# Rotary tables moved behind the first z tile, values stored by heads, unit weights loaded in halves, store waits moved

## What is computed

```
h = rmsnorm(x, pre_norm_w)                            # 2048 x 1024
q, k, v, z_att, b, c, u, z_conv, g_att, g_conv = split(h @ w_in)
q, k = partial_rotary(q, positions), partial_rotary(k, positions)   # 8 heads of 64, first 16 dims turned
a = softmax(q1 k1^T / 8) - lam * softmax(q2 k2^T / 8)  # 4 head pairs, chunk-causal mask (positions // 64)
att = rmsnorm(a @ v) * 0.8 * silu(z_att)               # v: 4 heads of 128
cv = b * conv3_causal(c * u) * silu(z_conv)
m = sigmoid(g_att + bias0) * (att @ w_att_out) + sigmoid(g_conv + bias1) * (cv @ w_conv_out)
x = x + rmsnorm(m @ w_out, post_norm_w)
```

## Time and profile before

| what | value |
|---|---|
| median of three executions | 1808.36 us (1807.6 to 1809.15) |
| the profiled execution | 1808.52 us |
| its span, first to last instruction | 1806.7 us |
| PE matmul busy | 1758.4 us, 97% of the span |
| PE weight load, DVE, ACT, POOL busy | 1466.7, 893.8, 580.3, 89.0 us |
| mean granted TensorE clock | 0.991 of full speed |
| DMA | 328.90 MB, mean 182 GB/s |
| PE's waits, largest groups | 12.4 us for `at_lo`, 11.1 us for unit weights, 8.1 us for the first x tile |

### The profile page before, as it was taken

One profiled execution on the slowest core, in us unless ns is written; L12 is line 12 of the kernel. 1 busy time (PEld: TensorE's weight loads), 2 busy tenths in 40 slices (PEclk: granted clock), 3 DMA queues, 4 the chain that ended last, 5 costly groups with the idle time before them and its releaser, 6 DMA issues.

```text
span 1806.7 us, 22424 instructions
## 1 busy us (share of the span) xinstructions
PE 1758.4 (97%) x8512; PEld 1466.7 (81%) x8512; DVE 893.8 (49%) x1903; ACT 580.3 (32%) x1039; POOL 89.0 (5%) x74
## 2 busy tenths in 40 slices
PE   7999999999999999999999999999899889999998
PEld 6887888888888888788887888888788768888887
DVE  5547244445334511276666666766576344424242
ACT  5423112121101111245444544444444333313231
POOL 0000000000000000111101111111001000000000
PEclk9999999999999999999999999999999999999999
DMA  6557346465503546965674778556856775453532
GB/s 233 164 189 314 129 163 210 163 210 167 178 18 129 162 118 174 265 219 186 198 211 151 221 233 271 181 180 208 248 158 185 227 281 172 120 181 111 175 105 76
DMA packets 149574, 328.90 MB, mean 182 GB/s; under 512 B 14801, under 2 KB 68049, under 8 KB 135889
## 3 DMA queue, kind: packets, MB, share of 16 engines
q1 hardware_dynamic: 149458, 327.37, 57.3%
HBM read 216.16 MB, written 111.16 MB: 181 GB/s over the span
## 4 chain that ended last, share of the span: by engine, by line
PE 83%; DMA 7%; ACT 3%; SPq 3%; DVE 2%; issue 2%; DVEq 0%; ACTq 0%
PE bank L937 18%; PE bank L938 18%; PE bank L939 18%; PE bank L1065 15%; PE bank L1027 5%; PE bank L999 3%; PE bank L1000 3%; PE bank L1010 2%; DMA raw<-in_w_in 2%; DMA ring<-gate_s 2%; SPq L669 2%; ACT e L1267 2%; DMA w<-split_s 1%; DMA gate_s<-gate_st 1%; DVE at_lo L1616 1%
## 5 line engine op out<-in xcount | busy, mean ns | idle before, releaser
L937 PE MATMUL bank<-ht,w 128*128 128x512 f32 x896 | 349.9, 390 | 3.0 <-issue 3.0
L938 PE MATMUL bank<-ht,w 128*128 128x512 f32 x896 | 349.7, 390 | 0.0
L939 PE MATMUL bank<-ht,w 128*128 128x512 f32 x896 | 349.5, 390 | 0.0
L1065 PE MATMUL bank<-ht,w 128*128 128x512 f32 x912 | 238.8, 396 | 4.0 <-DMA w<-split_s 4.0
L937 PEld LDWEIGHTS bank<-ht,w 128*128 128x128 f32 x896 | 168.8, 188 | 38.7 <-issue 3.4
L939 PEld LDWEIGHTS bank<-ht,w 128*128 128x128 f32 x896 | 168.9, 188 | 35.2
L938 PEld LDWEIGHTS bank<-ht,w 128*128 128x128 f32 x896 | 168.9, 188 | 35.1
L1065 PEld LDWEIGHTS bank<-ht,w 128*128 128x128 f32 x912 | 167.2, 189 | 36.7 <-DMA w<-split_s 4.6
L1580 DVE CUSTOM_DVE_ANT_0 e<-bank,zeros 128x512 f32<-128x512 f32 x192 | 125.0, 688 | 131.0 <-PE bank L1000 130.5
L1267 ACT ACTIVATE e<-e,nbias 128x128 f32<-128x128 f32 (+15 forms) x128 | 152.8, 1197 | 74.7 <-DVE nbias L1589 74.6
L1065 PE MATMUL bank<-hx,w 128*128 128x512 f32 x576 | 157.2, 401 | 7.0 <-DMA w<-split_s 7.0
(11 more groups left out here) (140 smaller groups left out, 2493.0 us busy)
## 6 DMA issues: line engine op xcount, KB each, us to landing
w<-split_s SPq DMA_DIRECT2D x62, 1024.0 KB, 5.4
split_s<-piece SPq DMA_DIRECT2D x24, 1024.0 KB, 5.0
q_st<-qk_s SPq DMA_DIRECT2D x128, 128.0 KB, 5.5
gate_s<-gate_st SPq DMA_DIRECT2D x64, 256.0 KB, 6.0
ring<-gate_s SPq DMA_DIRECT2D x64, 256.0 KB, 3.3
raw<-in_w_in SPq DMA_DIRECT2D x28, 512.0 KB, 5.7
ht_s<-ht SPq DMA_DIRECT2D x3, 4096.0 KB, 27.5
qk_s<-stage SPq DMA_DIRECT2D x48, 192.0 KB
```

The costliest lines, as they stand in the source:

```text
L937: nc.tensor.matmul(out, left[0], right[0], start=start, stop=False)
L938: nc.tensor.matmul(out, left[0], right[1], start=False, stop=False)
L939: return nc.tensor.matmul(out, left[1], right[0], start=False, stop=stop)
L1065: mm = nc.tensor.matmul(bank[2 + u % 2][:], unit_weights(u)[:, term // 2, k, :], h_slot(bb, k)[:, term % 2, :], start=i == 0, stop=i == PE ...
```

## The change

- DVE's table code becomes a function `tables()`, called in `before_tile(1)` after `tile_w(2)`; `chunk_ids()` moves to `before_tile(2)`. ACT's two sines move from `before_tile(0)` to `before_tile(1)`, after `tile_w(2)`.
- `v_s` becomes `[head, 128, row tile, hi/lo, 128]`. `stage` holds a v tile by heads, and a store writes runs of 1 KB instead of 2 KB. `load_v` is one DMA of 512 KB in which each partition reads one run of 4 KB, instead of two with 512-byte runs; `v_sl` has the matching order.
- A unit's weights come by two DMAs of 512 KB, k = 0 to 3 and k = 4 to 7, with a semaphore each. The first is issued when unit u - 2 is half done (new semaphore `unit_half`), the second when it is done. PE waits for the second only at its matmul 12.
- At the handover the load of unit 3 moves ahead of the last block's stores, the three further value loads move behind them, and the wait for all stores moves into the attention stage, to the end of unit 1, behind the store of unit 0.
- The first three `wa` loads are spread: behind units 49, 51 and 53.

```diff
-K_IN, V_IN, Q_IN = 2 * 16, 2 * 16, 4 * 16
+K_IN, V_IN, Q_IN = 2 * 16, 16, 4 * 16
-        v_s = scratch("v_s", [2, S, WIDTH])
+        v_s = scratch("v_s", [VH, P, NT, 2, VD])
-        v_sl = {i: held(f"v_sl{i}", [P, 2, QPB, VD], F32R, room) for i in (3, 0, 1, 2)}
+        v_sl = {i: held(f"v_sl{i}", [P, QPB, 2, VD], F32R, room) for i in (3, 0, 1, 2)}
+        def by_heads(i):
+            return stage[i % 4][:].rearrange("p s n -> p (s n)").rearrange("p (h s e) -> p h s e", h=VH, s=2)
-                sp.dma_start(v_s[:, i * P:(i + 1) * P, :].rearrange("s p e -> p s e"),
-                             stage[i % 4][:]).then_inc(stored[i % 4], 16)
+                sp.dma_start(v_s[:, :, i].rearrange("h p s e -> p h s e"), by_heads(i)).then_inc(stored[i % 4], 16)
-                for half in range(2):
-                    sp.dma_start(v_sl[i][:, half].bitcast(F32),
-                                 v_s[half, c:c + BLK, pair * VD:(pair + 1) * VD].rearrange("(t p) e -> p t e", p=P)
-                                 ).then_inc(v_loaded[i], 16)
+                sp.dma_start(v_sl[i][:].bitcast(F32), v_s[pair, :, c // P:c // P + QPB]).then_inc(v_loaded[i], 16)
-            def load_unit(u):
+            def load_unit(u, half=None):
                 if u >= 4:
-                    sp.wait_ge(unit_done, u - 1)
-                sp.dma_start(unit_weights(u)[:].bitcast(F32),
-                             split_s[u % GATE_TILES].rearrange("p s (k c) -> p s k c", k=KT)
-                             ).then_inc(first_in[u] if u < 2 else unit_w[u % 2], 16)
+                    if half:
+                        sp.wait_ge(unit_done, u - 1)
+                    else:
+                        sp.wait_ge(unit_half, u - 1)
+                for x in range(2) if half is None else (half,):
+                    sp.dma_start(unit_weights(u)[:, :, 4 * x:4 * x + 4].bitcast(F32),
+                                 split_s[u % GATE_TILES].rearrange("p s (k c) -> p s k c", k=KT)[:, :, 4 * x:4 * x + 4]
+                                 ).then_inc(first_in[u] if u < 2 else unit_w[2 * (u % 2) + x], 16)
             for i, (p, b) in enumerate(SEQ[-2 * NB:]):
+                if i == 7:
+                    sp.wait_ge(proj_done, AT[LINE - 1, 0] + 1)
+                    load_unit(3)
                 store_block(p, b)
...
                 if i == 6:
                     sp.wait_ge(proj_done, AT[LINE - 2, 0] + 1)
                     load_unit(2)
-                    for c in range(BLK, S, BLK):
-                        load_v(Plan(True), 0, c)
-            sp.wait_ge(proj_done, AT[LINE - 1, 0] + 1)
-            load_unit(3)
-            for i, s_ in enumerate(stored):
-                sp.wait_ge(s_, 16 * stored_in_all(i))
+            for c in range(BLK, S, BLK):
+                load_v(Plan(True), 0, c)
...
+                    if i == PER_UNIT // 2 - 1 and 4 <= u + 2 < UNITS:
+                        load_unit(u + 2, 0)
                     if i == PER_UNIT - 1:
                         if 4 <= u + 2 < UNITS:
-                            load_unit(u + 2)
+                            load_unit(u + 2, 1)
                         if u >= 1:
                             store_gate(u - 1)
+                        if u == 1:
+                            for x, s_ in enumerate(stored):
+                                sp.wait_ge(s_, 16 * stored_in_all(x))
                         if g % 2 == 1 and g < 12 and bb < NB - 1:
                             load_h(bb + 1, g // 2)
-                        if u == 3 * GATE_TILES + 1:
-                            for m in range(3):
-                                load_wa(m)
+                        if bb == NB - 1 and g in (1, 3, 5):
+                            load_wa(g // 2)
...
-                                pe.wait_ge(unit_w[u % 2], 16 * (u // 2))
+                                pe.wait_ge(unit_w[2 * (u % 2)], 16 * (u // 2))
...
+                        if i == PER_UNIT // 2 and u >= 2:
+                            pe.wait_ge(unit_w[2 * (u % 2) + 1], 16 * (u // 2))
...
-                        if i == PER_UNIT - 1:
+                        if i == PER_UNIT // 2 - 1:
+                            mm.then_inc(unit_half, 1)
+                        elif i == PER_UNIT - 1:
                             mm.then_inc(unit_done, 1)
...
             # ACT, before_tile(p)
-                if p == 0:
+                if p == 1:
                     act.wait_ge(cols_in, 48)
                     act.wait_ge(table_step, 14)
...
             # DVE, before_tile(p)
                 if 0 < p < LINE - 1:
                     tile_w(p + 1)
                 if p == 1:
+                    tables()
+                elif p == 2:
                     chunk_ids()
```

More of the change, by code:

```diff
@@ L471, in build @@
         att_stored = [sem(f"att_stored{i}") for i in range(2)]
-        unit_w = [sem(f"unit_w{i}") for i in range(2)]
+        unit_w = [sem(f"unit_w{i}") for i in range(4)]
         first_in = [sem(f"first_in{i}") for i in range(2)]
         ht_in = [sem(f"ht_in{i}") for i in range(KT // 2)]
-        ht_free, unit_done, gate_out = sem("ht_free"), sem("unit_done"), sem("gate_out")
+        ht_free, unit_half, unit_done, gate_out = sem("ht_free"), sem("unit_half"), sem("unit_done"), sem("gate_out")
         gate_stored = [sem(f"gate_stored{i}") for i in range(2)]
@@ L1025, in step @@
                         q0 = P if plan.causal and k == last else 0
-                        v = v_sl[plan.slot(G, k * P // BLK * BLK)][:, x // 2, k % QPB, :]
+                        v = v_sl[plan.slot(G, k * P // BLK * BLK)][:, k % QPB, x // 2, :]
                         return nc.tensor.matmul(bank[7][:, q0:QB], v, (at_lo if x == 1 else at_hi)[:, k, q0:QB],
@@ L1057, in gates @@
                             if u < 2:
-                                pe.wait_ge(first_in[u], 16)
+                                pe.wait_ge(first_in[u], 32)
                             else:
-                                pe.wait_ge(unit_w[u % 2], 16 * (u // 2))
+                                pe.wait_ge(unit_w[2 * (u % 2)], 16 * (u // 2))
                             if u >= 2:
                                 pe.wait_ge(gate_out, u - 1)
+                        if i == PER_UNIT // 2 and u >= 2:
+                            pe.wait_ge(unit_w[2 * (u % 2) + 1], 16 * (u // 2))
                         if bb and g == 0 and term == 0 and k % 2 == 0:
@@ L1185, in _ @@
                     act.wait_ge(stored[i % 4], 16 * (i // 4))
-                nc.scalar.activation(stage[i % 4][:, 0, :].bitcast(F32R), bank[4 + i % 4][:], ACT.Copy
+                nc.scalar.activation(by_heads(i)[:, :, 0].bitcast(F32R),
+                                     bank[4 + i % 4][:].rearrange("p (h e) -> p h e", h=VH), ACT.Copy
                                      ).then_inc(v_hi_out, 1)
@@ L1403, in _ @@
                 dve.wait_ge(v_hi_out, i + 1)
-                nc.vector.tensor_tensor(stage[i % 4][:, 1, :].bitcast(F32R), bank[4 + i % 4][:],
-                                        stage[i % 4][:, 0, :], ALU.subtract).then_inc(dve_done, 1)
+                nc.vector.tensor_tensor(by_heads(i)[:, :, 1].bitcast(F32R),
+                                        bank[4 + i % 4][:].rearrange("p (h e) -> p h e", h=VH),
+                                        by_heads(i)[:, :, 0], ALU.subtract).then_inc(dve_done, 1)
                 if i + 2 < NT:
```

29 lines of the change are left out of this document (15 added, 14 removed).

## The result

The changed kernel takes 1813.16 us, the median of seven executions (1810.76 to 1816.82). The kernel before took 1808.36 us in the seven beside them (1805.87 to 1809.77). The ratio is 1.0032 with a 95% interval of [1.0021, 1.0044]: slower by 0.32%, some 5 us. Forecast were 1806.8 us and no change, so it came out slower where no change was forecast, and the median lies 0.16 us above the top of the range. The profiled execution took 1813.16 us, with a span of 1811.3 us and a granted clock of 0.992.

A forecast was written before the change was run, and what follows sets the result against it. PE's matmuls fill 97% of the span, so only its stalls and lower clock could pay. Tables 13.5, v stores 0.5, gains 5.6, 2.4, 4.2 and 3.9, halves 0.5 sum to -1.6 us: 1806.8 us, 80% range 1798.5 to 1813.

The forecast's parts named there:

- tables: Before tile 3: PE stands 10.5 us behind DVE's moved table code, plus 3.0 us for the clock; cost 13.5 us.
- halves: Unit loads split in two: 60 more issues and later q, z and k loads; cost 0.5 us (0 to 2).
- B: Handover, units 2 and 3: idle plus clock 6.7 us, 1.1 us of stall left; gain 5.6 us (1 to 6.7).
- E: Unit 62: idle 2.80 us plus clock 1.5, in all 4.3; stall 0.4 left, gain 3.9 us (2.3 to 4.3).
- D: Change of keys, rounds 49 and 50: 5.9 us, stall 1.65 left, no clock fall; gain 4.2 us (2.8 to 5.9).
- Stores of v in 1 KB rows: Last v store, ahead of the raw tile on the queue: cost 0.5 us for tile 2 (0 to 1).
- second rival: Tables hidden after all, if tile 2's raw weights landed well before 160: -22.2 us, 1786; chance 0.07.
- A: Start of tile 2: idle 3.04 us plus clock 3.0, in all 6.0 us; gain forecast as nothing.
- third rival: Handover: SP's new wait for the `stage` stores makes q tiles late; total +5 us, 1813.4 us; chance 0.16.
- C: Change of keys, rounds 17 and 18: 4.1 us, stall 1.65 left, no clock fall; gain 2.4 us (1.2 to 4.1).
- first rival: Boundaries B to E clear whole, restart at tile 3 costs 1.2 us: -9.3 us, 1799.1 us; chance 0.31.
- The fourth: Clock falls in C and D as well and the halves cost SP 2 us: +2.5, up to +4; chance 0.05.

The follow-up runs named there:

- a3: The changed kernel with the load of tile 2's raw weights moved ahead of the three `ht` stores: 1793.65 us, ratio 0.9932 to the kernel before.
- b1: The changed kernel with tables, sines and `chunk_ids` at their old places and whole 1 MB unit loads: 1797.94 us, ratio 0.9954 to the kernel before.
- c1: The kernel before with only the unit loads in halves: 1809.56 us against 1805.92, ratio 1.0023.
- a2: The kernel before with only the tables, sines and `chunk_ids` moved to their new places: 1820.03 us, ratio 1.0073.
- a4: The kernel before with only the load of tile 2's raw weights moved ahead of the `ht` stores: 1804.01 us, ratio 0.9987.
- b3: The kernel before with only the handover's moves (unit 3's load, value loads, the wait for the stores): 1802.8 us, ratio 0.9983.
- b2: The kernel before with only the values stored by heads and one load per 512 keys: 1799.34 us, ratio 0.9959.
- a1: The changed kernel with tables, sines and `chunk_ids` back at their old places: 1800.61 us, ratio 0.9966 to the kernel before.
- c3: The changed kernel with tile 2's raw weights loaded ahead of the `ht` stores, halves throughout, run again: 1794.97 us, ratio 0.9940 to the kernel before.

## Why the prediction went wrong, point by point

From the profiles the change came out at +4.5 us where -1.6 was forecast. The cost of the tables was right to 0.6 us. Two steps failed. The halves were put at 0.5 us and cost 2.8 in one round that the sum did not contain. And the gains at B to E were put at 16.1 us and came to 11.7: a gate store that lands late, which the prediction took to be in time once SP comes earlier, held ACT at B, D and E, and E was priced from one profile.

**The tables: right.** Forecast: no gain at tile 2, a gap of 10.5 us before tile 3, PE back at 198, and 3.0 us for the clock. Measured: 10.00 us and 198.16. The 20-us stretches of the changed kernel (columns as in the earlier trace rows):

```profile
180.00:200.00 20.00, 10.00 (x41) 7.91 (x40) 12.68 (x17) 10.56 (x11) 0.00 (x0) 0.83 0.19 58
200.00:220.00 20.00, 20.00 (x83) 16.36 (x82) 11.56 (x15) 4.05 (x6) 0.00 (x0) 0.92 0.75 270
...
740.00:760.00 20.00, 18.80 (x87) 15.59 (x86) 3.68 (x15) 4.23 (x10) 1.57 (x1) 1.00 1.05 316
...
960.00:980.00 20.00, 18.15 (x107) 15.83 (x106) 11.47 (x32) 9.54 (x16) 1.57 (x1) 0.91 0.38 109
...
1300.00:1320.00 20.00, 17.52 (x110) 15.17 (x109) 11.03 (x31) 10.29 (x17) 1.57 (x1) 1.00 0.43 131
```

The clock cost 10.00 x 0.17 + 20.00 x 0.08 = 3.3 us where I had 3.0. Stores of v in 1 KB rows: tile 2 starts at 163.38 instead of 162.55, so 0.8 us for the 0.5 that I allowed. These readings add up to 14.1 us and the series has 13.4, where 14.0 was forecast. The second rival fell here for the reason given, and a3 shows that it hung on exactly that load. (Its sum had a slip: the terms of the prediction with A's 6.0 us and without the tables give -21.1 us, not -22.2.)

**The halves: the first step that failed.** I priced them at +0.5 us (0 to 2) and named the right mechanism (SP stops at every half unit, and what stands behind goes out later), but placed its cost nowhere. It falls in round 33, where keys, values, q tiles and unit weights are all loaded at once. SP's timeline of the changed kernel there:

```profile
1086.64 1.33 SPq L665 DMA_DIRECT2D k_sl<-qk_s  x2
1088.47 0.54 SPq L691 DMA_DIRECT2D w<-split_s  x1
1089.06 2.56 SPq L678 DMA_DIRECT2D q_st<-qk_s  x4
```

SP's timeline of the kernel before, the same q tiles:

```profile
1079.88 2.57 SPq L678 DMA_DIRECT2D q_st<-qk_s  x4
```

With the changed kernel 7.8 us behind, that is 1087.7 on its clock. They go out 1.4 us later, and the last of them takes 10.43 us to land (1091.01 to 1101.44), as PE's wait of 2.10 us shows, against 9.0 us in the kernel before. With the wait for `at_lo`, 1.57 us where it was 1.03, this is 2.6 us more idle time; by the series the round costs 2.8 us more than before, alone over the upper bound of the whole term. Whether SP's stop at the half unit or the smaller pieces ahead in the queue delay these tiles more, no run separates. Round 32 to 34 is no change of all four blocks of keys, so I never looked there. My list of places A to E was made of stalls that the kernel before *had*; a part that delays SP needs the places where it is only just in time.

The second half of the failed step is the reading of the earlier trace rows, "the second half is no later than the whole was". Both medians are over the whole span, quiet stretches included, and the 5.7 us are those of another load, the raw weights. The halves' own median is no worse (4.9 us in the changed kernel, 5.4 for whole loads before), yet where it counted it was: at the handover the first half of unit 2 took 14.7 us to land, the whole unit before 14.2. A half has 256 runs of 2 KB where the whole had 128 of 8 KB, and the page counts 164678 packets for 139079 with whole loads (b1). c1 measures all of it at +0.23% [0.14, 0.32], some 4 us. The Trainium skill (DMA: Bandwidth & Descriptors, Bandwidth) says to batch to 1 MiB or more. c1 agrees with it in direction, though it does not show that the size of the transfers is the cause, and the medians of the trace misled me. The estimate of 2.0 us by that page of the Trainium skill stood at E, while the loss that the traces show is in round 33.

**B: right in kind, 1.3 us too good.** Unit 3's wait is gone. But the order on SP is not what I drew. SP's timeline of the changed kernel at the handover:

```profile
742.65 8.54 SPq L691 DMA_DIRECT2D w<-split_s  x4
751.23 2.40 SPq L640 DMA_DIRECT2D qk_s<-stage  x3
...
756.41 0.33 SPq L730 DMA_DIRECT2D gate_s<-gate_st  x1
762.63 0.32 SPq L734 DMA_DIRECT2D hx<-ht_s  x1
763.00 0.54 SPq L691 DMA_DIRECT2D w<-split_s  x1
763.58 2.56 SPq L678 DMA_DIRECT2D q_st<-qk_s  x4
```

Four half loads held SP for 8.54 us, where a whole unit took 0.43 us to issue and units 2 and 3 as whole loads in b1 2.93 us. The DMA share of this stretch is 1.05, so I read it as SP being held by a full queue; that is argued, not shown. I had counted unit 2's wait out, because its first half would land 1.5 us before a whole one. But it landed 14.7 us after its issue at 742.65, and PE waits 1.20 us for it, where it had waited 0.55 for the whole. The last stores go out at 751, and SP waits for them until 762.63, 5.9 us. This is the place of the third rival. Less the 13.4 us that the changed kernel is behind, the landing is at 749.2: later than the 748 of the forecast, short of the 750.5 from which the rival decides, and PE did not stand for q at all. What was late is the row in between: the gate store of unit 0, issued at 756.41, landed 10.61 us later behind all this. From the chain of the changed kernel:

```profile
756.41 10.61 DMA gate_s<-gate_st
```

ACT's copy of unit 2 at 767.10, and its exponentials behind it, waited for that: 0.89 us before the first values. Idle left at B is 1.20 + 0.89 = 2.1 us, the clock stayed at 1.00 (row 740), and 6.7 - 2.1 = 4.6 agrees with the 4.3 of the series. I had left 1.1 us.

**C and D: mechanism right.** The weight waits are gone in both, `v_sl` went from eight issues in 7.40 us to four in 2.3 and 2.5 us, and the wait of 1.65 us for the exponentials came as forecast but longer: 1.85 and 2.44. At C the clock fell with it (0.91 in the row of 960), which I kept only as a bound: 18.15 x 0.09 = 1.6 us. That leaves 3.5 of 4.1 us; the series gives a gain of 1.3, in either case less than 2.4. The reason I gave for "no fall", the nearest stall by length, failed at C, so that it came true at D was luck. At D it did not fall after 2.44 us (1.00 in the row of 1300): 5.9 - 2.44 = 3.5, and 3.9 by the series, of the 4.2 forecast. ACT's wait for the gate store did not go at D; it shrank from 6.42 to 2.55 us, and that is why 2.44 stand there: from ACT's copy to the first product with the values it is 5.70 us again (1298.29 to 1303.99), as it is 5.71 at C (958.13 to 963.84).

**E: 2.2 of 3.9, and not shown to be the change's.** Two stalls remain at unit 62, 1.07 and 0.93 us, where I left 0.4. ACT waited 4.56 us for a gate store there, the same cause as at B. The halves did shorten the wait for weights: it is 2.0 us or less in all kernels with halves here and 2.1 to 2.8 in all with whole loads. But the time is no better for it, as a2 and a4 show, which have whole loads and the old order and step by the same -2.1 us. The forecast had priced E at 2.80 us of idle and 1.5 us of clock, both from one profile of the kernel before. In a2 and a4 the same code stands 2.30 us and keeps a clock of 1.00. In b3, also unchanged there, it stands 2.42 us, the clock shows 0.91 again, and the step is -0.4. So nearly half of the price of E hung on a fall of the clock that comes in some executions and not in others.

**Sum.** Of the forecast, A was 0.6 us too dear, and B, C, D and E together 4.4 us too good (-11.7 for -16.1). The halves were 2.3 us too cheap in round 33. -1.6 - 0.6 + 4.4 + 2.3 = +4.5 us, which is the series' end. The first rival, boundaries that clear whole, fell everywhere on the same thing: exponentials or a gate store waited behind each. The third has the nearest number, 1813.4 us for 1813.16 measured, but by chance: its stall behind SP's wait never came. The fourth, "the clock falls in C and D as well and the halves cost SP 2 us", was worked out at +2.5 to +4 with a chance of 0.05, and is the one that came closest in what happened: the halves cost over 2 us and the clock fell in C, though not in D. Of the signs named in advance, the gap before tile 3 and the times for `v_sl` (0.5 to 0.6 us of SP each) came; the waits for `w` fell to 2.3 us, not to under 1. The likely cases shared a term, the halves, that I had bounded from a median instead of from the fullest stretch of the queue.

## What to carry to other kernels

Price a change that splits or delays a DMA queue's work where that queue is fullest and where a transfer is only just in time, not only where the kernel already stalls. Before moving work behind a load, see what that load stands behind: here moving one 512 KB load ahead of 12 MB of stores turned a loss of 0.3% into a gain of 0.7%. Before pricing a stall from a profile, take a second one: the price of E, 4.3 us above, was 2.3 in two runs with the same code there. When two releasers end within a microsecond of each other, taking one away gives almost nothing, and the pair the whole stall.

## What the hardware did that I had not expected

- The same DMA does not always cost SP the same. A half unit of 512 KB took between 0.62 and 3.69 us of SP at the handover (8.54 us for four, with a DMA share of 1.05) and 0.54 us in the median after it.
- A store of 256 KB took 10.61 us to land at the handover, where the median of its 64 issues is 5.0 us. It held ACT's copy of the gate unit after next for 4.66 us.
- Whether the granted clock falls at a stall did not follow from the stall's length: the stretch with 1.85 us shows 0.91, the one with 2.44 us 1.00. At unit 62, b2 and b3 both stand 2.42 us for the weights, and the 20 us around it show 1.00 in b2 and 0.91 in b3. Judging 1.65 us by the nearest stall in length was not sound.
- Two kernels with the same code up to the last projection tile, a1 and b1, differ at unit 0 by 2.5 us in their profiles (0.1 and 2.6 us ahead of before). a3 and c3 are one and the same kernel, and at the last unit their profiles lie 17.9 and 13.7 us ahead. Steps within a profile agree better, but not to better than 1 to 2 us: at D these two step by -4.0 and -2.7.
